# Post-norms of a two-block transformer kernel: a quarter of the residual added on TensorE, memory transposes in the product banks, final multiplications in another order

## The reference, cut to what matters

```python
def rmsnorm(x, g):
    xf = x.astype(jnp.float32)
    y = xf * lax.rsqrt(jnp.mean(xf * xf, axis=-1, keepdims=True) + EPS) * g.astype(jnp.float32)
    return y.astype(x.dtype)
...
        h = h + rmsnorm(m @ w_out[l], norm_mix_post[l])
        u2 = rmsnorm(h, norm_mlp_pre[l])
        a = jnp.square(jax.nn.relu(u2 @ w_up[l]))
        h = h + rmsnorm(a @ w_down[l], norm_mlp_post[l])
```

## Time and profile before

| | us |
|---|---|
| median of 3 executions (1504.89 to 1505.08) | 1504.89 |
| the profiled execution's own time | 1505.0 |
| its span | 1503.2 |
| TensorE busy (PE) | 1493.5 (99%) |
| VectorE busy (DVE) | 1023.0 (68%) |
| ScalarE busy (ACT) | 786.8 (52%) |
| GpSimd busy (POOL) | 57.0 (4%) |
| DMA engines busy, mean share | 52% |

### The profile page before, as it was taken

How to read it: one execution, slowest core, us unless ns; L and a number is a source line. 1 busy time by engine, 2 the same in 40 slices (tenths; PEclk the granted TensorE clock), 3 DMA queues, 4 the chain that set the end, 5 groups by cost and what they waited for, 6 DMA issues and landing times.

```text
span 1503.2 us, 20831 instructions
## 1 busy us (share of the span) xinstructions
PE 1493.5 (99%) x8106; PEld 1284.8 (85%) x8106; DVE 1023.0 (68%) x1107; ACT 786.8 (52%) x903; POOL 57.0 (4%) x83
## 2 busy tenths in 40 slices
PE   9999999999999999999999999999999999999998
PEld 8878888888888888889888888888888888888886
DVE  5666766667666677987666667666567896676656
ACT  5654644446444465656544445444446655554444
POOL 0200100001000000010100001000000010000000
PEclk9999999999999999999999999999999999999999
DMA  9546455454555554353555455555545354355553
GB/s 373 204 148 236 176 196 189 174 196 170 194 195 180 212 196 172 137 196 112 196 196 194 172 195 196 204 184 195 196 170 201 134 196 168 112 200 192 194 191 118
DMA packets 40507, 280.44 MB, mean 187 GB/s; under 512 B 4608, under 2 KB 4864, under 8 KB 7040
## 3 DMA queue, kind: packets, MB, share of 16 engines
q1 hardware_dynamic: 39440, 275.08, 51.2%
q10 hardware_dynamic: 1008, 4.53, 0.8%
HBM read 277.49 MB, written 2.10 MB: 186 GB/s over the span
## 4 chain that ended last, share of the span: by engine, by line
PE 97%; DVE 1%; ACT 1%; issue 0%; POOL 0%; POOLq 0%; DVEq 0%; ACTq 0%
PE ps L396 95%; PE ps L638 1%; PE ps L630 1%; PE ps L692 0%; DVE w_lo L1557 0%; PE ps L1005 0%; ACT w_hi L1056 0%; DVE res L1889 0%; PE ps L620 0%; ACT Pb L1109 0%; ACT scratch L1093 0%; DVE Vx L1863 0%; DVE Vx L1731 0%; DVE Pb L1590 0%; POOL stat L2270 0%
## 5 line engine op out<-in xcount | busy, mean ns | idle before, releaser
L1557 DVE TENSOR_TENSOR w_lo<-raw,w_hi 128x2048 fp32r<-128x2048 f32 x250 | 571.4, 2290 | 246.1 <-ACT w_hi L1056 245.8
L1056 ACT ACTIVATE w_hi<-raw 128x2048 fp32r<-128x2048 f32 x251 | 479.9, 1915 | 284.0 <-PE ps L396 273.6
L396 PE MATMUL ps<-xT,w_hi 128*128 128x512 f32 (+1 forms) x2424 | 581.2, 383 | 0.0
L396 PEld LDWEIGHTS ps<-xT,w_hi 128*128 128x128 f32 x2424 | 436.2, 189 | 78.9 <-issue 0.2
L396 PEld LDWEIGHTS ps<-xT,w_lo 128*128 128x128 f32 x2304 | 311.0, 191 | 17.0
L396 PE MATMUL ps<-xT,w_lo 128*128 128x256 f32 x2304 | 320.9, 282 | 0.0
L396 PE MATMUL ps<-w_hi,sT_hi 128*128 128x512 f32 x576 | 186.2, 391 | 0.0
L396 PE MATMUL ps<-w_lo,sT_hi 128*128 128x512 f32 x576 | 185.5, 390 | 0.0
L396 PE MATMUL ps<-w_hi,sT_lo 128*128 128x512 f32 x576 | 185.4, 389 | 0.0
L396 PE MATMUL ps<-w_hi,xT 128*128 128x512 f32 x576 | 173.4, 392 | 0.1
L396 PEld LDWEIGHTS ps<-w_hi,xT 128*128 128x128 f32 x576 | 107.7, 188 | 24.3 <-issue 2.0
(11 more groups left out here) (203 smaller groups left out, 939.3 us busy)
## 6 DMA issues: line engine op xcount, KB each, us to landing
raw<-stream_in SPq DMA_DIRECT2D x255, 1024.0 KB, 4.8
raw<-stream_in SPq DMA_DIRECT2D x4, 256.0 KB, 5.4
kTx<-mem_in SPq DMA_DIRECT2D x1, 1024.0 KB, 12.2
cu<-gate_bias_in SPq DMA_DIRECT2D x1, 1024.0 KB, 14.1
qk_tok<-post_gain_in ACTq DMA_DIRECT2D x1, 1024.0 KB, 6.4
kTx<-mem_in ACTq DMA_DIRECT2D x1, 1024.0 KB, 6.6
mem_kept<-kTx ACTq DMA_DIRECT2D x1, 1024.0 KB, 4.0
kTx<-mem_kept ACTq DMA_DIRECT2D x1, 1024.0 KB, 4.8
```

The costliest lines, as they stand in the source:

```text
L396: return nc.tensor.matmul(bank_ap, lh, rh, start=start, stop=stop)
L1056: nc.scalar.activation(w_hi[:, slot(c), 0:width], raw[:, slot(c), 0:width], copy).then_inc(unit_hi, 1)
L1557: nc.vector.tensor_tensor(w_lo[:, slot(c), :], raw[:, slot(c), :], w_hi[:, slot(c), :].bitcast(F32), sub).then_inc(unit_lo, 1)
```

## The change: what it does

Five things change in a post-norm's seam, for both n:

1. Quarter 2 (half 0 of token tile 1) is no longer added by DVE before it is turned. TensorE makes its turned sum itself: `res[:, 1, k].T @ ident` (the old residual, 4 fp32 matmuls that open an accumulation), and later `Pb[:, 2, k].T @ factor` (4 fp32 matmuls that add to it), with `factor` the identity times the inverse root of token tile 1, a diagonal. These are ordinary fp32 matmuls of 128 columns, not transposes. `factor` is made by one ACTIVATE of 128x128 on ACT.
2. The memory's 8 transposes move behind the first four of `res` and the four identity matmuls, and write banks 4 and 6 in place of 2 and 3.
3. The matmul without use in front of `turn_post` goes.
4. DVE adds quarter 3 right after it has scaled it; quarter 2 is added to `res` (512 columns in one) only after `turn_rest`, ahead of `rest_unit` of the next product's second unit. ACT's squares of the whole `res` get a wait for it.
5. In `keep_mem` ACT makes `factor` between its two copies.

At the end of the program two of the three `gained` multiplications each move one quarter later. The diff:

```diff
@@ -45,7 +45,7 @@
 F_COLS = KT * 2 * HEADS
 F_STEP, F_LOW = 64, 32
 
-WARM_X, WARM_FIRST, WARM_NORM = 4, 2, 1
+WARM_X, WARM_FIRST = 4, 2
 UNIT = 2048
 RING = 3
 TRI = 3 * P
@@ -160,6 +160,7 @@
         xmax = sb("xmax", [P, 2, 8])
         rinv = sb("rinv", [P, 16])
         bcol = sb("bcol", [P, 1])
+        factor = sb("factor", [P, P])
         bpick = sb("bpick", [P, HEADS])
         cT = sb("cT", [P, S], F32R)
 
@@ -242,7 +243,7 @@
         rstd = sem("rstd")
         sel_ready = sem("sel_ready")
         post_rstd = sem("post_rstd")
-        post_piece = sem("post_piece")
+        factor_ready = sem("factor_ready")
         mem_T, mem_ready, mem_saved = sem("mem_T"), sem("mem_ready"), sem("mem_saved")
         cols_ready = sem("cols_ready")
 
@@ -642,17 +643,23 @@
 
             def turn_post(n):
 
-                warm(WARM_NORM)
+                half_of = lambda k: ps[:, U[k // 2], (k % 2) * S + P:(k % 2) * S + 2 * P]
                 pe.wait_ge(res_ready, 4 * n + 1)
                 turn_part(res, U, 0, 0, (0, 4))
-                pe.wait_ge(post_piece, n + 1)
-                turn_part(res, U, 0, 1, (0, 2))
+                for k in range(4):
+                    mm(half_of(k), res[:, 1, k * P:(k + 1) * P], ident, k % 2 == 0, False)
+                turn_mem(n)
+                pe.wait_ge(res_ready, 4 * n + 2)
+                turn_part(res, U, 1, 0, (0, 4))
+                pe.wait_ge(b_dve.sem, BB(("postmixb", "postmlpb")[n]))
+                pe.wait_ge(factor_ready, n + 1)
+                for k in range(4):
+                    last = mm(half_of(k), Pb[:, 2, k * P:(k + 1) * P], factor[:], False, k % 2 == 1)
+                    if k % 2 == 1:
+                        last.then_inc(turn_T, 1)
                 pe.wait_ge(res_ready, 4 * n + 3)
-                turn_part(res, U, 0, 1, (2, 4))
+                turn_part(res, U, 1, 1, (0, 4))
                 pe.wait_ge(mem_ready, n + 1)
-                turn_part(res, U, 1, 0, (0, 4))
-                pe.wait_ge(res_ready, 4 * n + 4)
-                turn_part(res, U, 1, 1, (0, 4))
 
             def turn_res(banks, before):
 
@@ -667,7 +674,7 @@
                     pe.wait_ge(mem_in, 32)
                 for k in range(4 * half, 4 * half + 4):
                     for t in range(TOK):
-                        last = nc.tensor.transpose(ps[:, 2 + (k % 4) // 2, (k % 2) * S + t * P:(k % 2) * S + (t + 1) * P],
+                        last = nc.tensor.transpose(ps[:, 4 + 2 * ((k % 4) // 2), (k % 2) * S + t * P:(k % 2) * S + (t + 1) * P],
                                                    mem_tok[:, t, k * P:(k + 1) * P], ident)
                 last.then_inc(mem_T, 1)
 
@@ -796,7 +803,6 @@
                     mixed_turned(3)
 
 
-            turn_mem(0)
             turn_post(0)
 
             def up(r3, c, jr, j, tiles=None):
@@ -832,7 +838,6 @@
                     up(r * 4, c, r * 3, b + 2)
                     down1(r * 4, c + 2, r * 3, b + 1, SQ_TILE[(b + 2) % 3])
             down1(0, c0 + 30, 0, 7, SQ_TILE[2], stop=True)
-            turn_mem(1)
             turn_post(1)
 
 
@@ -1095,10 +1100,14 @@
 
             def keep_mem(half):
 
+                def kept(a):
+                    return nc.scalar.activation(mem_tok[:, a, half * 512:half * 512 + 512], ps[:, 4 + 2 * a, :], copy)
+
                 act.wait_ge(mem_T, half + 1)
-                for a in range(2):
-                    last = nc.scalar.activation(mem_tok[:, a, half * 512:half * 512 + 512], ps[:, 2 + a, :], copy)
-                last.then_inc(mem_ready, 1)
+                kept(0)
+                act.wait_ge(post_rstd, post_done(half, 1))
+                nc.scalar.activation(factor[:], ident, copy, scale=rs(T_MIX, 1)).then_inc(factor_ready, 1)
+                kept(1).then_inc(mem_ready, 1)
 
             def probs(hp):
 
@@ -1237,6 +1246,7 @@
             turn_round(2 * BT, U, colsA[:, C_MLPPRE:C_MLPPRE + KT])
             c0 = B1_UNITS - B1_MLP
             round_unit(0, c0 + 2)
+            act.wait_ge(res_ready, 4)
             squares(res_t, T_FFN, 8)
 
             def sq_round(jr, j, tile):
@@ -1306,6 +1316,8 @@
                     g = colsL[:, (L_FFN1, L_FFN2)[which]:][:, 0:KT]
                     turn_round(turns_before(l, 0 if which == 0 else 5), U, g)
                     round_unit(L3, base + 2)
+                    if l == 0 and which == 0:
+                        act.wait_ge(res_ready, 8)
                     squares(res_t, T_FFN, sums_of(l, (0, 3)[which]) - 2)
 
                     def gate(jr, j):
@@ -1771,10 +1783,10 @@
                     return nc.vector.tensor_tensor(Pb[:, q, :], ps[:, 4 + 2 * half + t, :],
                                                    gain[:, half * 512:half * 512 + 512], mul)
 
-                def onto(q, c0=0, c1=512):
+                def onto(q):
                     half, t = BY_TOKEN[q]
-                    r = res[:, t, half * 512 + c0:half * 512 + c1]
-                    return stt(out=r, in0=Pb[:, q, c0:c1], scalar=rs(T_MIX, t), in1=r, op0=mul, op1=add)
+                    r = res[:, t, half * 512:half * 512 + 512]
+                    return stt(out=r, in0=Pb[:, q, :], scalar=rs(T_MIX, t), in1=r, op0=mul, op1=add)
 
                 dve.wait_ge(gpost_in, 16)
                 scaled(0)
@@ -1787,12 +1799,12 @@
                 did1(scaled(3), f"{name}b")
                 dve.wait_ge(post_rstd, post_done(n, 1))
                 wait_own1(f"{name}b")
-                onto(2, 0, 256).then_inc(post_piece, 1)
-                onto(2, 256, 512).then_inc(res_ready, 1)
                 onto(3).then_inc(res_ready, 1)
-
-            post_norm(0, gpost[:, 0:D], "postmix", 4)
+                return lambda: onto(2).then_inc(res_ready, 1)
+
+            quarter_left = post_norm(0, gpost[:, 0:D], "postmix", 4)
             turn_rest(2 * BT, U, colsA[:, C_MLPPRE:C_MLPPRE + KT])
+            quarter_left()
             c0 = B1_UNITS - B1_MLP
             rest_unit(0, c0 + 1)
             rest_unit(0, c0 + 2)
@@ -1850,7 +1862,7 @@
                     if b == 1:
                         sq_rest(r * 3, b + 2, SQ_TILE[b])
                     rest_unit(r * 4, c + 6)
-            post_norm(1, gpost[:, D:2 * D], "postmlp", 10)
+            quarter_left = post_norm(1, gpost[:, D:2 * D], "postmlp", 10)
             b_dve.closed()
 
 
@@ -1888,13 +1900,15 @@
                         r = res[:, t, half * 512:half * 512 + 512]
                         stt(out=r, in0=ps[:, base + 2 * half + t, :], scalar=scale(t), in1=r, op0=mul,
                             op1=add).then_inc(res_ready, 1)
-                        if i == 4 and l == LAYERS - 1 and q < 2:
-                            gained(q)
+                        if i == 4 and l == LAYERS - 1 and q in (1, 2):
+                            gained(q - 1)
 
                 def ffn(which, base):
                     fb = l * (2 * FB)
                     f0 = which * FB
                     turn_rest(turns_before(l, 0 if which == 0 else 5), U, colsL[:, (L_FFN1, L_FFN2)[which]:][:, 0:KT])
+                    if l == 0 and which == 0:
+                        quarter_left()
                     rest_unit(L3, base + 1)
                     rest_unit(L3, base + 2)
```

## The result

| | us |
|---|---|
| before, median of 20 executions (1504.66 to 1505.08) | 1504.89 |
| changed, median of 20 executions (1507.42 to 1508.02) | 1507.74 |
| ratio, with its 95% interval | 1.0019 (1.0013 to 1.0025) |
| the profiled execution's own time, changed | 1507.64 |
| its span | 1505.8 |

The changed kernel is 2.85 us slower, 0.19%. The interval lies wholly above 1, so the change makes the kernel slower; the size is just under the 0.2% that I had set as the line, and the interval reaches across that line. The forecast was 1507.5.

The account below looks back on a forecast made before the run. TensorE, busy 1493.5 of 1503.2 us, was taken to bound the kernel. Seams of +1.55 and +1.6 and -0.6 at the end sum to +2.55 on the profiled 1505.0: 1507.5 us, range 1505.4 to 1509.2.

Parts of the forecast that it names:

- case A: The forecast itself: ACT's first copy holds `factor` back, each seam grows 1.5 to 1.6 us; 1507.5 us, chance 0.70.
- Step 5: `factor` on ACT, behind the first memory copy: ends at 159.89, TensorE starts at 159.95 after idling 0.7 us.
- Step 6: Two products with `factor`, then ACT's first pair of roundings at 160.65 instead of 159.53: 1.12 us late.
- Steps 1 to 4: TensorE's seam work ahead of `factor`: quarter 0's transposes, identity matmuls, memory's transposes, quarter 1's transposes, from 156.60 to 159.23.
- Step 2: Four identity matmuls on TensorE in the seam, 0.22 us each, 0.88 us together, without a wait.
- rival B: Ordinary fp32 products against an identity take 0.43 us each, eight 3.4 us per seam; 1510.1 us, chance 0.11.
- Step 7: Behind the seam, the postponed 0.71 us addition delays the unit's rest for the second unit: 0.43 us more on the path.
- Step 8: Behind the seam, ACT's squares wait for the postponed addition until about 165.4; costed at nothing because ACT is rounding until then.
- Even with no wait at all the new seam would be as long as the old: TensorE's own work in a seam rises from 3.04 to 3.94 us; the old seam with its holes is 3.92.
- Both lines are tight: Old seam: the chain over ACT's roundings to `turn_hi`, at about 160.35, and TensorE's own 16 transposes end at the same time.
- The end: End of the program: quarter 2's addition at 1494.7 instead of 1495.78, ACT's last squares at 1496.8; 0.6 us less.
- rival D: TensorE's clock falls from 2.4 to 1.2 GHz in each seam, 5.6 us per seam; over 1516 us, chance 0.02.

Follow-up runs that it names:

- Run 3: Changed kernel with quarter 2's addition on DVE taken back to right behind quarter 3's, after a wait for the memory's transposes: 1506.79 us.
- run 8: Changed kernel reordered: DVE makes `factor`, memory's transposes first, quarter 1's transposes behind `factor`'s products, quarter 2 added early: 1504.66 us.
- Runs 4: Changed kernel with both `factor` ahead of ACT's two copies and quarter 2's addition early on DVE: 1505.24 us.
- Run 9: Kernel before with final-gain multiplications later, memory's transposes in banks 4 and 6, quarter 1's transposes before quarter 2's wait, no matmul without use: 1504.22 us.
- run 6: Kernel before without the matmul without use: 1504.85 us, beside 1504.87 for the kernel before.
- run 5: Changed kernel with the matmul without use put back in front of each seam's turn: 1508.56 us.
- run 7: Kernel before with only the two final-gain multiplications moved one quarter later: 1504.28 us, beside 1504.92.
- runs 1 and 2: Changed kernel, first with `factor` made before ACT's two copies: 1506.11 us; second, instead, with the memory's transposes ahead of the identity matmuls: 1506.01 us.

## Why the prediction was right, point by point

- **The number, case A, 1507.5:** measured 1507.74, inside the range and within 0.3 of the number; less than the 0.2% line, as I held likeliest. The terms measured sum to +2.79 where I had +2.55: what is short lies in the two seams (steps 5 and 6), and 0.1 of it was made good by chance, since I started from the profiled 1505.0 and not from the median 1504.89.
- **Steps 1 to 4, TensorE up to `factor`:** I had 2.63 us from the first record to the end of quarter 1's transposes, it is about 2.68 (156.40 to 159.08). Step 2: 0.225 per fp32 matmul of 128 columns, against the 0.22 read from the few early ones (there are four such distances in that trace, from 25.37, 25.84, 26.31 and 26.78, all 0.22, where I counted two). That was the figure on which most hung, and rival B falls with it. The rule of the Trainium skill that I set against it ("TensorE: Matmul & The Clock Gate", Terms) does not hold here: 0.225 against 0.109 us is a factor of 2, not of 4.
- **Step 5, who is waited for:** the copy starts 2.45 us into the seam (I had 2.40), `factor` 0.49 behind it and 0.39 long as taken. The term that was too small is the way from ACT to TensorE: 159.73 to 159.88, 0.15 us, where I had used the 0.06 between DVE and TensorE. The wait is 0.63 us by the waits view, TensorE's empty stretch 0.8.
- **Step 6:** the first roundings are late by 160.60 - 159.53 = 1.07, and since the seam started 0.2 earlier on the trace's time axis, by 1.27 within the seam; I had 1.12. The 0.15 too little are the 0.09 of step 5 and 0.05 in the start of the copy.
- **Step 7, the second unit:** 0.41 and 0.48, forecast 0.43 and about 0.5. Run 3 shows that it is the addition. That the number fits so well is partly luck, since two small errors cancel: the addition pushes the unit's rest back by 0.66 (164.61 to 165.27), not 0.71, and of the 0.3 I took for slack 0.05 is the way from DVE to the weights (the rest ends at 165.27 + 2.29 = 167.56, the weights start at 167.61), so only 0.25 could be used up.
- **Step 8, the wait of ACT's squares:** it cost nothing, but only just. In n = 0 the addition is over at 164.61 + 0.74 = 165.35, and the squares start at 165.39, when ACT has finished rounding the next unit. With the addition early (run 3) the gain was no more than the second unit's wait, within 0.1 us.
- **"Even with no wait at all the new seam would be as long as the old":** run 8 is that seam, 4.08 against 3.92. Runs 4 and 8 together say that arranging it better recovers 2.5 to 3.1 us and ends level, with the end's 0.6 us included. Of the old seam I had said "Both lines are tight". Run 9 takes 0.43 us off TensorE's line and the length stays, so the line over ACT was enough to set it.
- **The removed matmul:** in the old seam it was worth nothing, as run 6 shows, and run 5 shows what it would have cost on the new path.
- **The end:** 0.64, forecast 0.6; alone, in run 7, 0.6.
- **The clock (rival D):** nothing of it. Run 6 has a hole of 1.1 us and the same distances as before, and the granted clock of the changed kernel was 0.999 over the span, as before, and 1.00 in every two microseconds of both seams. By the Trainium skill, "TensorE: Matmul & The Clock Gate", Part 1, a gate sets the clock by how busy TensorE has been recently; in the seams of this kernel, with holes of up to 1.1 us, the trace shows no fall.

Why the seam grew, in one sentence: the change replaced a chain of DVE's piece of 0.48 us and two transposes by an ACTIVATE and two matmuls of twice a transpose's price behind the same inverse root, so that nothing was won even without a wait, and it bound the ACTIVATE to TensorE's own list by way of the memory's copy. The first half of the sentence is shown by run 8, the second by runs 1 and 2.

What stays open: whether `factor`'s products in another number format would make the scheme a gain; it was not tried, and it would change the precision of the residual.

## What to carry to other kernels

A wait that one engine takes away must be followed to what stands ahead of the new producer in its own list: here ACT sat idle with the input of `factor` on hand, since a copy that waited for something later stood first. Before buying a wait off with extra work on the bounding engine, compare the engine's own work in the new stretch with the length of the old stretch including its hole; where they are equal, the best that can come out is nothing. And a short hole on the bounding engine is only room if what ends it does not depend on that engine: the same 0.43 us cost 0 in the one kernel and 0.4 per seam in the other.

## What the runs showed of the hardware that I had not expected

- An ACTIVATE's result reached TensorE 0.12 to 0.15 us after the record's end (159.73 to 159.85 for the weights and 159.88 for the matmul), a DVE addition's in about 0.06 (158.99 to 159.05 before). I had taken one figure for both. The matmuls that wait differ too (ordinary fp32 ones here, transposes there); but a DVE rest reached ordinary weights in 0.05 (167.56 to 167.61), which points to the engine that sends. No run tests it by itself.
- A fp32 matmul of 128 columns against the identity costs 0.225 us between starts, in two records, and a transpose of the same size 0.109, in one (changed kernel, seam n = 0).
- DVE makes a 128x128 diagonal from the identity in 0.28 us where ACT takes 0.39 (run 8 and the changed kernel).
